# State-space stage: one decay matrix for both directions by a predicated copy, step sizes as logarithms, one product per head on unweighted rows

## What is computed

```python
dt_f = jax.nn.softplus(dt_f_raw + dtb[0]); dt_b = jax.nn.softplus(dt_b_raw + dtb[1])
y_f, s_f = ssd_chunked(x, dt_f, A[0], B, C, init_f)
y_b, s_b = ssd_chunked(x[:, ::-1], dt_b[:, ::-1], A[1], B[:, ::-1], C[:, ::-1], init_b)
y = y_f + y_b[:, ::-1] + d_skip[:, None] * x

# in ssd_chunked
acum = cumsum(dt * A)                                     # per chunk and head
seg = where(causal, acum[..., :, None] - acum[..., None, :], -inf)
cb = einsum('bcign,bcjgn->bcgij', C, B)                   # shared by the 8 heads of a group
y_diag = einsum('bcghij,bcjghp->bcighp', cb * exp(seg), x * dt)
chunk_states = einsum('bcghj,bcjgn,bcjghp->bcghpn', exp(acum[..., -1:] - acum), B, x * dt)
S_final, S_in = lax.scan(step, init_state, (chunk_states, exp(acum[..., -1])))
y_off = einsum('bcign,bcghpn,bcghi->bcighp', C, S_in, exp(acum))
```

## Time and profile before

| | us |
|---|---|
| median of 3 runs (1596.34 to 1596.6) | 1596.5 |
| the profiled execution | 1595.94 |
| its span | 1594.0 |
| PE busy | 1497.1 (94%) |
| DVE busy | 892.9 (56%) |
| ACT busy | 672.9 (42%) |
| POOL busy | 141.7 (9%) |
| mean granted clock of PE | 0.977 of full speed |

### The profile page before, as it was taken

How to read it: one execution, slowest core, us unless ns; L and a number is a source line. 1 busy time by engine, 2 the same in 40 slices (tenths; PEclk the granted TensorE clock), 3 DMA queues, 4 the chain that set the end, 5 groups by cost and what they waited for, 6 DMA issues and landing times.

```text
span 1594.0 us, 21345 instructions
## 1 busy us (share of the span) xinstructions
PE 1497.1 (94%) x8533; PEld 1360.7 (85%) x8533; DVE 892.9 (56%) x1453; ACT 672.9 (42%) x1148; POOL 141.7 (9%) x126
## 2 busy tenths in 40 slices
PE   6889798999999999999997897999999999999998
PEld 2779576888899999999986896777888999999998
DVE  2697354465456554554536974455644656465562
ACT  2534453445354433343425444445335445343341
POOL 0010200344000000000000102015320000000000
PEclk9899899899999999999999997999999999999999
DMA  9446563232434455565645341221425333343440
GB/s 330 138 132 211 160 201 95 64 93 67 119 116 137 159 186 197 174 210 172 219 141 152 90 119 53 80 67 54 117 68 145 107 119 119 120 131 120 127 125 40
DMA packets 186089, 210.23 MB, mean 132 GB/s; under 512 B 10702, under 2 KB 154374, under 8 KB 185990
## 3 DMA queue, kind: packets, MB, share of 16 engines
q1 hardware_dynamic: 185990, 208.86, 42.3%
HBM read 204.90 MB, written 3.93 MB: 131 GB/s over the span
## 4 chain that ended last, share of the span: by engine, by line
PE 85%; DVE 9%; ACT 3%; issue 2%; POOL 1%; DMA 1%; SPq 0%; DVEq 0%; ACTq 0%; POOLq 0%
PE bank L636 22%; PE bank L637 21%; PE bank L638 21%; PE y_ps L880 3%; PE bank L650 2%; PE bank L651 2%; PE bank L652 2%; DVE tb L1507 2%; PE y_ps L691 1%; PE bank L668 1%; DVE wlo L1411 1%; PE seg_ps L668 1%; PE seg_ps L770 1%; PE y_ps L889 1%; PE y_ps L902 1%
## 5 line engine op out<-in xcount | busy, mean ns | idle before, releaser
L1411 DVE TENSOR_TENSOR wlo<-raw,whi 128x1024 fp32r<-128x1024 f32 (+1 forms) x288 | 353.0, 1233 | 247.5 <-ACT whi L1044 246.3
L636 PE MATMUL bank<-ahi,whi 128*128 128x384 f32 (+1 forms) x1280 | 446.3, 349 | 6.8 <-DVE wlo L1411 6.8
L637 PE MATMUL bank<-alo,whi 128*128 128x384 f32 (+1 forms) x1280 | 437.2, 342 | 0.0
L638 PE MATMUL bank<-ahi,wlo 128*128 128x384 f32 (+1 forms) x1280 | 436.7, 341 | 0.0
L1044 ACT CAST whi<-raw 128x1024 fp32r<-128x1024 f32 (+1 forms) x288 | 296.2, 1036 | 330.2 <-PE bank L638 180.0
L636 PE MATMUL bank<-bhi,whi 128*128 128x384 f32 x768 | 264.4, 344 | 8.0 <-DVE arena_g L1616 4.7
L636 PEld LDWEIGHTS bank<-ahi,whi 128*128 128x128 f32 x1280 | 244.9, 191 | 21.4 <-issue 11.8
L637 PE MATMUL bank<-blo,whi 128*128 128x384 f32 x768 | 259.3, 338 | 0.0
L638 PE MATMUL bank<-bhi,wlo 128*128 128x384 f32 x768 | 259.3, 338 | 0.0
L637 PEld LDWEIGHTS bank<-alo,whi 128*128 128x128 f32 x1280 | 244.9, 191 | 2.9 <-issue 2.4
L638 PEld LDWEIGHTS bank<-ahi,wlo 128*128 128x128 f32 x1280 | 244.5, 191 | 0.0
(11 more groups left out here) (220 smaller groups left out, 1481.3 us busy)
## 6 DMA issues: line engine op xcount, KB each, us to landing
raw<-in_w_mlp_dram SPq DMA_DIRECT2D x128, 512.0 KB, 3.6
raw<-in_w_in_dram SPq DMA_DIRECT2D x104, 512.0 KB, 3.7
raw<-in_w_mod_dram SPq DMA_DIRECT2D x96, 512.0 KB, 6.2
raw<-in_w_ssd_o_dram SPq DMA_DIRECT2D x16, 512.0 KB, 3.5
raw<-in_w_out_dram SPq DMA_DIRECT2D x16, 512.0 KB, 3.5
raw<-in_w_pool_o_dram SPq DMA_DIRECT2D x8, 512.0 KB, 3.5
raw<-in_w_attn_o_dram SPq DMA_DIRECT2D x8, 512.0 KB, 3.4
raw<-in_w_in_dram SPq DMA_DIRECT2D x8, 256.0 KB, 3.3
```

Source lines behind the costliest of these rows:

```text
L636: nc.tensor.matmul(dst, uh[:, k, tm_cols(m)], hi[k0 + k], start=first and k == 0, stop=False)
L637: nc.tensor.matmul(dst, uh[:, k, tm_cols(m)], lo[k0 + k], start=False, stop=False)
L638: ins = nc.tensor.matmul(dst, ul[:, k, tm_cols(m)], hi[k0 + k], start=False, stop=last and k == 3)
L1411: nc.vector.tensor_tensor(rest, full, top.bitcast(F32), ALU.subtract).then_inc(lo_ready, 1)
```

## The change

The weights of both directions now stand in one matrix per tile: above the diagonal the forward decay, below it the backward one. ACT copies the forward differences from `seg_ps` to `ew` (`seg_copy`), PE then writes the backward ones to `seg_ps`, and DVE takes them over where j > i by a predicated copy under a constant mask (`pick`). One exponential (`seg_exp`) and one product with unmasked C·B (`weigh`) follow. The logarithm of the step size is added to the exponent: six more products on PE, with `ident`, of slots that hold the negated logarithms, add it to the rows that `seg` reads; ACT takes the logarithm and DVE fills the slots at the end of `softplus`. So `ydiag` multiplies x itself, and once per tile. The backward term on the diagonal goes into the skip weights: `skip_columns` (DVE) multiplies C·B's diagonal by the backward steps and adds d_skip, and `skip_rows` (POOL) writes x times these to `dtx`, to which `y_diag` adds `ybank`. The fillers move between slots, and the steps are in another order on PE, ACT, DVE and POOL.

```diff
...
-SSD_SLOTS = ((2, 1, 1, 0, 1, 0, 1, 0, 0, 1, 0, 1, 0), (1, 1, 1, 1, 1, 0, 1, 0, 0, 1, 0, 1, 0))
+SSD_SLOTS = ((2, 1, 1, 1, 0, 1, 0, 0, 0, 1, 0, 1, 0), (1, 1, 1, 1, 1, 1, 0, 0, 0, 1, 0, 1, 0))
...
     for i in range(6):
-        ins = nc.tensor.matmul(seg_ps[:, i // 4, tm_cols(i % 4)], adt_slots[:, tm_cols(i)], tri[i % 2], start=True, stop=True,
+        ins = nc.tensor.matmul(seg_ps[:, i // 4, tm_cols(i % 4)], adt_slots[:, tm_cols(i)], tri[i % 2], start=True, stop=False,
+                               skip_group_check=True)
+        ins = nc.tensor.matmul(seg_ps[:, i // 4, tm_cols(i % 4)], log_slots[:, tm_cols(i)], ident, start=False, stop=True,
                                skip_group_check=True)
     ins.then_inc(acsT_done, 1)
...
                                    spread[part, i % 2].rearrange("p h i -> p (h i)"), start=True, stop=True)
         ins.then_inc(seg_done, 1)
-    def ydiag(g, t, e):
-        pe.wait_ge(w_ready, (l * 2 + g) * 6 + 2 * t + e + 1)
-        if e == 0:
-            pe.wait_ge(dtx_ready, (l * 2 + g) * 3 + t + 1)
-            if t or g:
-                pe.wait_ge(y_free, (l * 2 + g) * 3 + t)
+    def ydiag(g, t):
+        pe.wait_ge(w_ready, (l * 2 + g) * 3 + t + 1)
+        if t or g:
+            pe.wait_ge(y_free, (l * 2 + g) * 3 + t)
         for h in range(HG):
-            ins = nc.tensor.matmul(ybank[:, h * 64:h * 64 + 64], ew[:, e, h, :], dtx[:, e, h * 64:h * 64 + 64],
-                                   start=h == 0 and e == 0, stop=h == 7 and e == 1, skip_group_check=True)
+            ins = nc.tensor.matmul(ybank[:, h * 64:h * 64 + 64], ew[:, (g + t) % 2, h, :],
+                                   xbuf[:, t, (g * HG + h) * 64:(g * HG + h) * 64 + 64], start=h == 0, stop=h == 7,
+                                   skip_group_check=True)
         ins.then_inc(ydiag_done, 1)
...
         seg(g, 1)
         fill(slot[1])
         transposes4(2, stage[:, 2])
-        ydiag(g, 0, 0)
         seg(g, 2)
         fill(slot[2])
-        ydiag(g, 0, 1)
+        ydiag(g, 0)
         state_sum(3, 2)
+        seg(g, 3)
         fill(slot[3])
         state_sum(4, 1)
-        seg(g, 3)
+        seg(g, 4)
         fill(slot[4])
         state_sum(5, 0)
-        ydiag(g, 1, 0)
         fill(slot[5])
         pe.wait_ge(stT_ready, (l * 2 + g) * 2 + 1)
         transposes4(6, stage[:, 0])
-        seg(g, 4)
+        ydiag(g, 1)
+        seg(g, 5)
         fill(slot[6])
-        ydiag(g, 1, 1)
         state_sum(7, 0)
         fill(slot[7])
         pe.wait_ge(stT_ready, (l * 2 + g) * 2 + 2)
         transposes4(8, stage[:, 0])
-        seg(g, 5)
         fill(slot[8])
-        ydiag(g, 2, 0)
         yoff(9, 1, 0, 0)
         fill(slot[9])
+        ydiag(g, 2)
         yoff(10, 1, 1, 3)
         fill(slot[10])
-        ydiag(g, 2, 1)
         yoff(11, 2, 0, 2)
         fill(slot[11])
         yoff(12, 2, 1, 1)
...
-    act.wait_ge(dt_step, l * 3 + 3)
+    act.wait_ge(dt_step, l * 4 + 3)
     nc.scalar.activation(dtl, dtw, ACT.Ln).then_inc(dt_act, 1)
+    act.wait_ge(dt_step, l * 4 + 4)
+    nc.scalar.activation(dtw, dtm, ACT.Ln).then_inc(dt_act, 1)
...
     nc.scalar.activation(wdec, dtm, ACT.Exp).then_inc(decay_ready, 1)
-    def seg_exp(g, i):
-        n = (l * 2 + g) * 6 + i + 1
-        act.wait_ge(seg_done, n)
-        if i >= 2 or g:
-            act.wait_ge(ydiag_done, (l * 2 + g) * 6 + i - 1)
-        rows = ew[:, i % 2].rearrange("p h i -> p (h i)")
-        nc.scalar.activation(rows, seg_ps[:].rearrange("p b n -> p (b n)"), ACT.Relu, scale=-1.0).then_inc(seg_taken, 1)
-        act.wait_ge(seg_taken, n)
-        nc.scalar.activation(rows, rows, ACT.Exp, scale=-1.0).then_inc(exp_ready, 1)
+    def seg_copy(g, t):
+        act.wait_ge(seg_done, (l * 2 + g) * 6 + 2 * t + 1)
+        n = g * 3 + t
+        if n >= 2:
+            act.wait_ge(ydiag_done, l * 6 + n - 1)
+        nc.scalar.copy(ew[:, (g + t) % 2].rearrange("p h i -> p (h i)"), seg_ps[:].rearrange("p b n -> p (b n)"))\
+            .then_inc(seg_taken, 1)
+    def seg_exp(g, t):
+        act.wait_ge(seg_taken, (l * 2 + g) * 6 + 2 * t + 2)
+        rows = ew[:, (g + t) % 2].rearrange("p h i -> p (h i)")
+        nc.scalar.activation(rows, rows, ACT.Exp).then_inc(exp_ready, 1)
...
         fill(slot[0])
+        seg_copy(g, 0)
+        keep(1, st[:, 0, :], st_ready, (l * 2 + g) * 2 + 1)
         seg_exp(g, 0)
-        keep(1, st[:, 0, :], st_ready, (l * 2 + g) * 2 + 1)
-        seg_exp(g, 1)
         fill(slot[1])
         keep(2, st[:, 1, :], st_ready, (l * 2 + g) * 2 + 2)
-        seg_exp(g, 2)
+        seg_copy(g, 1)
         fill(slot[2])
+        seg_exp(g, 1)
         fill(slot[3])
-        seg_exp(g, 3)
+        seg_copy(g, 2)
         fill(slot[4])
         keep(5, stage[:, 0, :], stT_ready, (l * 2 + g) * 2 + 1)
         fill(slot[5])
         keep(6, stage[:, 1, :], state_staged, (l * 2 + g) * 2 + 1)
-        seg_exp(g, 4)
+        seg_exp(g, 2)
         fill(slot[6])
         keep(7, stage[:, 0, :], stT_ready, (l * 2 + g) * 2 + 2)
         fill(slot[7])
         keep(8, stage[:, 2, :], state_staged, (l * 2 + g) * 2 + 2)
-        seg_exp(g, 5)
         fill(sum(slot[8:]))
...
         link(nc.vector.scalar_tensor_tensor(dta, dtv, 0.0, dtl, ALU.max, ALU.add))
         link(nc.vector.scalar_tensor_tensor(by_t(adt), by_t(dta), -1.0, wide(dtf[:, 0:32]), ALU.mult, ALU.mult))
-        nc.vector.tensor_copy(adt_slots.rearrange("p (i s h) -> p i s h", s=8, h=4), adt.rearrange("p (i h) -> p i h", h=4)
-                              .unsqueeze(2).to_broadcast([P, 24, 8, 4])).then_inc(adt_ready, 1)
+        nc.vector.tensor_scalar(dtm, dta, 1.2e-38, None, ALU.max).then_inc(dt_step, 1)
+        nc.vector.memset(log_slots, 0.0)
+        each = lambda v, n: v.rearrange("p (i h) -> p i h", h=4).unsqueeze(2).to_broadcast([P, 24, n, 4])
+        link(nc.vector.tensor_copy(adt_slots.rearrange("p (i s h) -> p i s h", s=8, h=4), each(adt, 8)))
+        dve.wait_ge(dt_act, l * 4 + 4)
+        nc.vector.tensor_scalar(log_slots.rearrange("p (i s h) -> p i s h", s=8, h=4)[:, :, 2:4, :], each(dtw, 2), -1.0,
+                                None, ALU.mult).then_inc(adt_ready, 1)
...
-    def weigh(g, i):
-        t, e = i // 2, i % 2
-        dve.wait_ge(exp_ready, (l * 2 + g) * 6 + i + 1)
-        nc.vector.tensor_tensor(ew[:, e], ew[:, e], cbs[:, e, t, :].unsqueeze(1).to_broadcast([P, HG, P]), ALU.mult)\
+    def pick(g, t):
+        dve.wait_ge(seg_taken, (l * 2 + g) * 6 + 2 * t + 1)
+        dve.wait_ge(seg_done, (l * 2 + g) * 6 + 2 * t + 2)
+        nc.vector.copy_predicated(ew[:, (g + t) % 2], backward.unsqueeze(1).to_broadcast([P, HG, P]),
+                                  seg_ps[:].rearrange("p b (h i) -> p (b h) i", i=P)).then_inc(seg_taken, 1)
+    def weigh(g, t):
+        dve.wait_ge(exp_ready, (l * 2 + g) * 3 + t + 1)
+        rows = ew[:, (g + t) % 2]
+        nc.vector.tensor_tensor(rows, rows, cbs[:, t, :].unsqueeze(1).to_broadcast([P, HG, P]), ALU.mult)\
             .then_inc(w_ready, 1)
+    def skip_columns(g):
+        diag = tb[:, 3, 0:T].rearrange("p (t n) -> p t n", t=TT)
+        link(nc.vector.tensor_tensor(diag, cbs[:], ident.unsqueeze(1).to_broadcast([P, TT, P]), ALU.mult))
+        link(nc.vector.tensor_reduce(cb_diag[:], diag, AX_X, ALU.add))
+        back = dta.rearrange("p (t e h) -> p t e h", t=TT, e=2)[:, :, 1, g * 8:g * 8 + 8]
+        link(nc.vector.tensor_tensor(skips[:, g], back, cb_diag[:].unsqueeze(2).to_broadcast([P, TT, HG]), ALU.mult))
+        nc.vector.tensor_tensor(skips[:, g], skips[:, g], dskip[:, g * 8:g * 8 + 8].unsqueeze(1)
+                                .to_broadcast([P, TT, HG]), ALU.add).then_inc(skip_ready, 1)
...
-        dve.wait_ge(ydiag_done, (l * 2 + g) * 6 + 2 * t + 2)
-        nc.vector.tensor_tensor(xbuf[:, t, cols], xbuf[:, t, cols], ybank, ALU.add).then_inc(y_free, 1)
+        dve.wait_ge(ydiag_done, (l * 2 + g) * 3 + t + 1)
+        dve.wait_ge(dtxd_ready, (l * 2 + g) * 4 + (4, 2, 1)[t])
...
         fill(slot[0])
         dve.wait_ge(aux_done, (l * 2 + g) * 13 + 1)
         if g:
-            dve.wait_ge(w_ready, (l * 2 + g) * 6)
-        for e in range(2):
-            ins = nc.vector.tensor_tensor(cbs[:, e], aux[:, 0:T].rearrange("p (t n) -> p t n", t=TT),
-                                          tri[e].unsqueeze(1).to_broadcast([P, TT, P]), ALU.mult)
-        ins.then_inc(aux_free, 1)
+            dve.wait_ge(w_ready, (l * 2 + g) * 3)
+        nc.vector.tensor_copy(cbs[:], aux[:, 0:T].rearrange("p (t n) -> p t n", t=TT)).then_inc(aux_free, 1)
...
+        pick(g, 0)
+        skip_columns(g)
+        fill(slot[1])
         weigh(g, 0)
-        weigh(g, 1)
-        fill(slot[1])
-        weigh(g, 2)
+        pick(g, 1)
         fill(slot[2])
         next_state(g, 3, 2, 1, 1, 3)
         fill(slot[3])
+        weigh(g, 1)
+        y_diag(g, 0)
         next_state(g, 4, 1, 0, 0, 2)
-        weigh(g, 3)
-        y_diag(g, 0)
         fill(slot[4])
         fill(slot[5])
```

(15 more changed lines are left out.)

50 lines of the change are left out of this document (26 added, 24 removed).

## The result

The change is slower: 1621.9 us (median of 4 runs, 1620.3 to 1622.8) against 1596.55 us, a ratio of 1.0158 with a 95% interval of 1.014 to 1.0175. The forecast was 1616 us with a range of 1603 to 1627. The profiled execution has a span of 1620.9 us against 1594.0, 26.9 us more.

What follows compares the result with a forecast made beforehand. PE was taken to bound the kernel (85% of the span). Terms 7.2 (waits less removed products) + 2.4 + 4.3 + 0.2 (before the stage) + 5 (clock) made +19 us on 1595.9, so 1616 us for the median; range 1603 to 1627.

Steps and rivals of the forecast that it cites:

- What goes: Twelve of 24 `ydiag` groups leave PE's path at 1.73 us each: 20.8 us less.
- The predicated copy: DVE's `pick`, which had no row in the trace: taken as 1.25 us.
- Rival 2: The predicated copy takes 1.95 to 2.45 us and feeds stalls in eight places: 1622 to 1626 us; chance 0.16.
- New waits: PE's new waits for DVE and ACT in both groups: +7.2 us over two layers, in place of -20.8.
- step 8: Second `transposes4` of the state, all four groups: PE waits 2.35 us for ACT's copy in place of 0.8.
- the restarts: PE's restarts after waits: 0.2 us each, three more in group 0, four in group 1.
- Before the stage: Longer `softplus` on DVE +2.4 us, and six products with `ident` on PE +4.3 us, plus 0.2 for constants.
- The clock: Group 0's stall of 4.9 us makes the granted clock fall to 0.50: +5 us over two layers, between 0 and 9.
- Rival 1: The clock holds through group 0's stall: 1611 us; chance 0.2.
- Rival 4: DVE gets through its queue in less than PE's 5.7 us, so the 20.8 us arrive: 1582 us; chance 0.05.

Runs made afterwards that it cites:

- e7: e6 with, on PE, `seg(g, 5)` ahead of `state_sum(7)` and `ydiag(g, 1)` cut in two halves around the transposes of step 8; 1573.3 us.
- e4: The changed kernel without the logarithm of the step sizes (its six PE products, ACT's second logarithm, DVE's maximum, memset and slot product); 1619.1 us.
- e1: The changed kernel with ACT's `seg_exp(g, 2)` moved behind the copies of steps 7 and 8; 1606.5 us.
- e3: e1 plus, on DVE, `next_state(g, 4)` ahead of the filler of slot 3, `weigh(g, 1)` and `y_diag(g, 0)`; 1588.1 us.
- e6: e5 with DVE's `next_state(g, 3)` ahead of `pick(g, 1)` and slot 2's filler, `next_state(g, 4)` ahead of `weigh(g, 1)` and slot 3's filler; 1578.8 us.
- e8: The changed kernel with DVE's `next_state(g, 4)` ahead of `weigh(g, 1)` and `y_diag(g, 0)`, still behind the filler of slot 3; 1616.3 us.
- e5: e3 with `ydiag(g, 2)` behind `yoff(10)` on PE and `y_diag(g, 2)` behind `y_off(10)` on DVE, as before the change; 1587.3 us.

## Why the prediction was right, point by point

- **What goes.** -20.8 us forecast; -21.0 measured as PE's busy time in the stage (e7 against before).
- **The predicated copy.** 1.25 us taken, 1.32 measured. Rival 2 (1.95 to 2.45) falls.
- **New waits.** The places were all found. Before `state_sum(5)` 4.9 us forecast, 6.5 measured; group 1 1.8 + 0.9 forecast, 2.1 + 2.1 measured; step 8 2.35 and 2.13; `yoff(9)` 0.85 and 0.72; `yoff(11)` 0.8 and 0.85. With the restarts +28.0 us forecast (7.2 + 20.8); measured are 30.1 us of idle time and about 1.3 of restarts, which count as busy: 3.4 too little. Too short were the rows of DVE beside POOL; the text knew the 1.95 us row and did not put it into the walk.
- **Before the stage.** +6.9 forecast, +0.8 measured in the profiled executions, 2.1 to 2.8 by e4 for the logarithms alone. Layer 1 came out near its terms (1.2 and 1.4). In layer 0 the first probability transposes, said to come 1.2 us later, start at 183.72 us as against 183.73. The 2.9 us for six products in layer 0 was the price at 1.2 GHz times the old count; it did not add to the time, since the low stretch there ended earlier (286 us, against 291 before).
- **The clock: the step that failed.** "Every wait of PE longer than 3 us in this trace was met by a fall [...] Group 0's stall of 4.9 us is one such", +5 us. Measured: 15.7 at the lower level (17.0 with the restarts). The term was mis-sized because it priced one stall a layer: it took the shortest wait of 3 us or more that fell before the change (3.35) as a bound. The trace before already spoke against that on both sides. A low stretch at 905 to 912 us stood at two waits of 2.45 and 2.48 us, and one at 281 to 291 us had no wait longer than 1.6 us in the 90 us ahead of it; and the waits of 4.4 and 4.8 us at the launch were met by no fall (granted clock 1.00 up to 37 us). The change made eight waits of about 2.1 us, and the clock fell behind six of them. e1, e3 and e6, which remove some of them, got back more than their length; e8, which removes one a layer, did not. What these runs show is that the short waits count together with the long one; which of them the clock falls at stays open. Rival 1, that the clock holds, falls.
- **Faster.** Rival 4 named the right place, DVE's queue between `pick(g, 1)` and the second `next_state`, and the two copies. Its 1582 us lies between two orders in which these are mended, e5 (1587) and e6 (1579); in the kernel as changed the waits came, as the forecast had it.

+19 us was forecast and +25.4 measured (+26.9 in the profiled executions). There the terms miss by 10.7 us too little for the clock, 3.4 too little for waits and restarts, and 6.1 too much ahead of the stage. The direction and the places are the prediction's own; that 1621.9 lies within its range, 6 us above the forecast, is in part luck, since the last error cancels more than half of the largest.

## What to carry to other kernels

Taking work off the engine that bounds a kernel also takes cover off its waits: list, for each step behind which a product went, what it now asks for earlier, and walk that queue with the durations seen beside a busy POOL. Put what the bounding engine waits for (here `next_state` and the copies) ahead of what it doesn't ask for soon (a unit three ahead, a gate); the same instructions ran 49 us apart in two orders (1621.9 and 1573.3). Count the short waits of the bounding engine, here those of 2.1 us, as more than their length on the whole, without booking a gain for each one removed (e8), and price the clock from busy time of the same instructions in a stretch at 1.00.

## What was not expected of the hardware

- Waits of PE of 2.1 us were followed by low stretches with 3.4 us of matmuls, at some 1.7 us each (1.55 in e3). Not all: behind the one that ended at 382.37 us the clock stayed, and it fell at the next, at 390.43. Nor is one place the same in every run: both kernels wait 2.80 us, at 97.96 and 97.58 us, and do the same work there; before, and then after:

```profile
98.00:100.00 2.00, 2.00 (x11) 2.00 (x12) 2.00 (x2) 0.00 (x0) 2.00 (x2) 1.00 1.00 365
```

```profile
98.00:100.00 2.00, 2.00 (x9) 2.00 (x8) 2.00 (x2) 0.00 (x0) 2.00 (x2) 0.53 1.05 402
```

The granted clock, the column before the DMA share, is 1.00 in the one and 0.53 in the other. What decides it these runs don't show. "TensorE: Matmul & The Clock Gate" of the Trainium skill (section What's actually happening) has the throttle as the default state, released by activity; falls while PE is idle agree, and the two rows above say that the last wait's length alone does not settle it.

- A DVE operation with both operands in SBUF can be longer beside POOL, by up to 0.75 us whatever its own length: 1.22 to 1.95 for 1024 elements, 0.69 to 1.42 for 512, 0.26 to 0.9 for 96. How much depends on the moment. In the changed kernel, where POOL's operation had 0.87, 0.74 and 0.36 us left as DVE's began (at 320.37, 302.99 and 313.54 us), DVE's took 0.73, 0.61 and 0.22 us more; where DVE's began first, by 0.05 us, it took its plain 0.69 (at 322.95). POOL's rows for the first and the last of these:

```profile
319.89 1.35 POOL L1908 TENSOR_TENSOR arena_s<-xbuf,skips 128x512 f32<-128x512 f32 x1
323.00 1.55 POOL L1908 TENSOR_TENSOR arena_s<-xbuf,skips 128x512 f32<-128x512 f32 x1 [1.76 <-DVE xbuf L1719]
```

The predicated copy, with one operand in PSUM, took 1.33 to 1.34 us with POOL busy for all of it (at 299.58 and 312.31 us), 1.30 with POOL busy for part (335.19) and 1.29 with POOL idle (400.02). "SBUF — State Buffer" of the Trainium skill (section Who interferes with whom) has one port pair shared by the two engines, taken as an exclusive lock; a delay that does not grow with DVE's operation, but follows what is left of POOL's, agrees with that.

- Cut from the queue of one engine, such a delay comes out at the operation that takes its place (e8): the cost belongs to the moment, not to the operation.
